# Two-layer hybrid block on one Trainium2 core: openings of both attentions and of S5's output rearranged

## What is computed

```python
# first block: one input projection, three branches, a gated merge, an MLP
proj = einsum('bld,dn->bln', rmsnorm(x), w_in)
y_a = s5_mixer(u_s5, ...)            # 32 groups: complex scan, gelu, sigmoid gate
y_b = short_conv_mixer(...)
y_c = forgetting_attention(q, k, v, f_logit, b_f)  # 8 heads, cum = cumsum(log_sigmoid(f + b_f))
merged = sum(gate_n * (y_n @ w_branch_n))
x = x + rmsnorm(merged @ w_out)
x = x + rmsnorm(square(relu(h @ w_ff1)) @ w_ff2)
# second block: one input projection, four branches, a gated merge, a SwiGLU MLP
o_a = chunk_band_attention(aq, ak, av, rel_bias)    # 4 heads, window of 576 keys
o_b = hgrn2(...);  o_c = spatial_gating(...);  o_d = rg_lru_branch(...)
```

## Time and profile before

| | |
|---|---|
| time, median of 3 executions | 3750.2 us (3750.17 to 3753.09) |
| the profiled execution | 3750.94 us, span 3749.2 us |
| TensorE matmul busy | 3518.4 us, 94% of the span |
| TensorE weight load busy | 2823.8 us, 75% |
| VectorE, ScalarE, GpSimd busy | 1434.4, 874.2, 893.5 us (38%, 23%, 24%) |
| mean granted clock of TensorE | 0.974 |
| low part of one weight unit on GpSimd (L270) | 2.48 us, mean of 276 |
| one issue of a `dl` DMA on SP (L1132) | 0.64 to 3.27 us, median 1.76 |
| issue of the first sixteen `s5_uc` loads on SP | from 88.0 us, 8.60 us long |

### The profile page before, as it was taken

How to read it: one execution, slowest core, us unless ns; L and a number is a source line. 1 busy time by engine, 2 the same in 40 slices (tenths; PEclk the granted TensorE clock), 3 DMA queues, 4 the chain that set the end, 5 groups by cost and what they waited for, 6 DMA issues and landing times. The chain is left out here.

```text
span 3749.2 us, 40647 instructions
## 1 busy us (share of the span) xinstructions
PE 3518.4 (94%) x16120; PEld 2823.8 (75%) x16120; DVE 1434.4 (38%) x1582; ACT 874.2 (23%) x1068; POOL 893.5 (24%) x421
## 2 busy tenths in 40 slices
PE   7986999999998999999988998899999899999996
PEld 4865887887885888888866887677777678888885
DVE  7713466654425212222152445562453522121123
ACT  3112222223323111111131222212232311111111
POOL 1101111111341222222321223331244222222223
PEclk9988999999999999999998999999999999999998
DMA  3335334324432111111223323213254111111122
GB/s 113 97 63 193 116 111 152 96 90 152 148 110 73 51 45 50 45 51 45 90 89 103 108 74 113 73 57 134 93 179 158 68 50 50 45 45 51 45 78 101
DMA packets 105120, 337.85 MB, mean 90 GB/s; under 512 B 15264, under 2 KB 25376, under 8 KB 104880
## 3 DMA queue, kind: packets, MB, share of 16 engines
q1 hardware_dynamic: 103520, 331.35, 27.0%
q10 hardware_dynamic: 1472, 4.72, 0.3%
HBM read 251.42 MB, written 88.67 MB: 91 GB/s over the span
## 5 line engine op out<-in xcount | busy, mean ns | idle before, releaser
L270 POOL TENSOR_TENSOR w_lo<-w_raw,w_hi 128x1024 fp32r<-128x1024 f32 x276 | 684.6, 2480 | 2502.4 <-ACT w_hi L268 2502.4
L305 PE MATMUL pair<-act_hi,w_hi 128*128 128x512 f32 x3024 | 984.5, 407 | 15.1 <-issue 7.0
L305 PE MATMUL pair<-act_lo,w_hi 128*128 128x512 f32 x3024 | 955.8, 397 | 0.0
L305 PE MATMUL pair<-act_hi,w_lo 128*128 128x512 f32 x3024 | 953.8, 396 | 0.0
L305 PEld LDWEIGHTS pair<-act_lo,w_hi 128*128 128x128 f32 x3024 | 572.4, 189 | 140.0
L305 PEld LDWEIGHTS pair<-act_hi,w_lo 128*128 128x128 f32 x3024 | 570.5, 189 | 139.9
L305 PEld LDWEIGHTS pair<-act_hi,w_hi 128*128 128x128 f32 x3024 | 553.1, 190 | 143.4 <-issue 16.5
L268 ACT CAST w_hi<-w_raw 128x1024 fp32r<-128x1024 f32 x276 | 288.9, 1047 | 770.8 <-PE pair L305 707.6
L580 DVE TENSOR_TENSOR p<-pair,rs 128x1024 f32<-128x1024 f32 x101 | 123.4, 1222 | 442.4 <-PE pair L305 436.3
L1780 DVE TENSOR_TENSOR f2v<-pair,rs 128x1024 f32<-128x1024 f32 x42 | 51.5, 1225 | 346.6 <-PE pair L305 346.6
L305 PE MATMUL pair<-f1hh,w_hi 128*128 128x512 f32 x480 | 147.8, 389 | 0.0
(11 more groups left out here) (462 smaller groups left out, 4041.5 us busy)
## 6 DMA issues: line engine op xcount, KB each, us to landing
w_raw<-in_stream SPq DMA_DIRECT2D x278, 512.0 KB, 3.6
proj<-p SPq DMA_DIRECT2D x101, 512.0 KB, 2.6
m2g<-proj SPq DMA_DIRECT2D x32, 512.0 KB, 4.8
foxx<-proj SPq DMA_DIRECT2D x32, 256.0 KB, 6.1
m1g<-proj SPq DMA_DIRECT2D x16, 512.0 KB, 3.3
x<-f1y SPq DMA_DIRECT2D x16, 512.0 KB, 2.6
act_lo<-x SPq DMA_DIRECT2D x16, 512.0 KB, 7.1
m1l<-mixed SPq DMA_DIRECT2D x12, 512.0 KB, 9.3
```

Source lines behind the costliest of these rows:

```text
L270: nc.gpsimd.tensor_tensor(wlo[:, slot, :], raw[:, slot, :], whi[:, slot, :].bitcast(F32), ALU.subtract).then_inc(s_split, 1)
L305: last = nc.tensor.matmul(out_pair[:, h * HALF:(h + 1) * HALF], wt, a[:, h * HALF:(h + 1) * HALF], start=k == 0 and n_pass == 0, stop=k == ...
```

## The change

- The copy of the input to `x0` is issued by SP within S5, right after the first sixteen loads of `s5_uc`; the two copies into spare rows are dropped, and so are the rows.
- Of the eight DMAs into `dl`, every second is issued by ScalarE (counted on `s5_in`), the others by SP, and `beside(14)` stands behind them instead of `beside(7)`.
- `beside(6)` is added ahead of the Gelus.
- `fetch(h)` waits for the three rows that it reads, not for twelve. Five points of tiles stand behind `fetch(0)` instead of two. For fox the number of points over which the tiles are spread stays `FOX_HEADS * 24 + 8`.
- In the second block 52 row blocks are one string; band begins after 25 tiles of it, without the two barriers, and its points are `BAND_HEADS * 24 + 9`. `edge` is added to the bias in `prepare(h)`. The small constants of HGRN's lower bound are made at head 2 instead of head 0.

```diff
-    def attention(heads, tiles, src, rows, mixed, row0, head_bias, add_bias, name, beside=None, closing=True):
+    def attention(heads, tiles, src, rows, stored, mixed, row0, head_bias, add_bias, name, beside=None, closing=True):
...
                 if h:
                     SP.wait_ge(*split[h - 1])
+                for n in range(3):
+                    SP.wait_ge(*stored[rows[n] + h // 2])
...
-                bias_ready[h] = bias_in(h)
+                bias_in(h)
...
                 split[h] = V.mark(V.after(a_k).tensor_tensor(ks[HD:P, sl, :], raw_qk[HD:P, 1, :],
                                                              ks[HD:P, sl, :].bitcast(F32), ALU.subtract))
+                bias_ready[h] = bias_fixed(h)
...
             fetch(0)
-            point(2)
+            point(5)
             prepare(0)
             point(2)
             state["copied"] = values(0, None)
...
-        for row in range(Q_, F_):
-            SP.wait_ge(*stored[row])
...
             edge = sb(outer, "bd_edge", [P, BAND])
-            barrier()
-
             G.mark(G.then().memset(edge[:], 0.0))
             G.mark(G.then().memset(edge[0:64, LEFT + 64:], -1e30))
-            G.mark(G.then().memset(edge[64:P, 0:64], -1e30))
-            barrier()
+            edged = G.mark(G.then().memset(edge[64:P, 0:64], -1e30))
+            G.then()
...
-                def ready(h):
-                    got = bias_load[h % 2].mark(SP.dma_start(rel[:, h % 2, :], t["rel"][h]))
-                    return V.mark(V.after(got).tensor_tensor(rel[:, h % 2, :], rel[:, h % 2, :], edge[:], ALU.add))
-                return rel, ready
+                def fetched(h):
+                    bias_load[h % 2].mark(SP.dma_start(rel[:, h % 2, :], t["rel"][h]))
+
+                def fixed(h):
+                    return V.mark(V.after(bias_load[h % 2].last(), edged).tensor_tensor(rel[:, h % 2, :], rel[:, h % 2, :],
+                                                                                        edge[:], ALU.add))
+                return rel, fetched, fixed
...
             chunks(0)
             chunks(1)
+            x0_out.mark(SP.dma_start(x0, x_in))
...
-            SP.wait_ge(*v)
-            SP.wait_ge(*zeroed)
+            for queue in (SP, nc.scalar):
+                queue.wait_ge(*v)
+                queue.wait_ge(*zeroed)
             for j in range(T):
-                dl_in.mark(SP.dma_start(dl[j * S5_H:(j + 1) * S5_H, :, j * S5_H:].rearrange("p g (a b) -> p g a b", b=S5_H),
-                                        kc[:, :, 0:T - j, :]))
-            w.beside(7)
+                queue, arrived = ((SP, dl_in), (nc.scalar, s5_in))[j % 2]
+                arrived.mark(queue.dma_start(dl[j * S5_H:(j + 1) * S5_H, :, j * S5_H:].rearrange("p g (a b) -> p g a b", b=S5_H),
+                                             kc[:, :, 0:T - j, :]))
+            w.beside(14)
...
             w.beside(5)
+            w.beside(6)
             gelus = [A.mark(A.after(u_in[n].last()).activation(z[n], z[n], ACT.Gelu_apprx_tanh)) for n in range(4)]
...
-            if head == 0:
+            if head == 2:
...
             w.upto(17 * KT + 1)
-            for spare, d in enumerate((proj1[N1], proj2[N2])):
-                stores[spare].mark(SP.dma_start(d, x_in[0]))
-            x0_copied = x0_out.mark(SP.dma_start(x0, x_in))
             w.again(FOX_HEADS * 24 + 8, KT)
...
-        stored = {}
-        stage(2, 2, 2, KT, act_rhs, to_dram(proj2, AQ + 2, buf), per=out_per)
-        barrier()
+        stored = {row: outs[row - AQ].last() for row in (AQ, AQ + 1)}
...
-        with Woven(products(0, used["units"], 48, 48, KT, act_rhs, evict), 48 * KT, 1) as w:
+        with Woven(products(0, used["units"], 52, 52, KT, act_rhs, evict), 52 * KT, 1) as w:
             with ExitStack() as early:
                 hgrn_const, constants_beside = hgrn_constants(early)
-                w.again(BAND_HEADS * 24 + 6, 32 * KT)
-                band(constants_beside)
+                w.upto(3 * KT + 1)
+                w.again(BAND_HEADS * 24 + 9, 32 * KT)
+                band(constants_beside, stored)
```

More of the change, by code:

```diff
@@ L669, in attention @@
             st = sb(at, name + "st", [P, 2, 1])
-            bias, bias_in = head_bias(at)
+            bias, bias_in, bias_fixed = head_bias(at)
             G.mark(G.then().memset(vt[:, :, 0, :, HD:], 1.0))
@@ L796, in head_bias @@
             cb = sb(at, "fx_cb", [P, 2, L])
-            return cb, lambda h: bias_load[h % 2].mark(SP.dma_start(cb[:, h % 2, :], fox_cum[h].partition_broadcast(P)))
+            def fetched(h):
+                bias_load[h % 2].mark(SP.dma_start(cb[:, h % 2, :], fox_cum[h].partition_broadcast(P)))
+            return cb, fetched, lambda h: bias_load[h % 2].last()
         def add_bias(sc, psum, cb, q0, k0, k1):
@@ L802, in add_bias, with band, fetched @@
             return v
[L804 to L805 removed]
         with ExitStack() as at:
[L807 removed]
+            attention(FOX_HEADS, [(n * P, 0, (n + 1) * P) for n in range(8)], proj1, (Q_, K_, V_), stored, mixed1, 8,
                       head_bias, add_bias, "fox", short_conv(at, stored), closing=False)
[L810 removed]
+    def band(beside, stored):
         with ExitStack() as outer:
             edge = sb(outer, "bd_edge", [P, BAND])
[L814 removed]
             G.mark(G.then().memset(edge[:], 0.0))
             G.mark(G.then().memset(edge[0:64, LEFT + 64:], -1e30))
[L818 to L819 removed]
+            edged = G.mark(G.then().memset(edge[64:P, 0:64], -1e30))
+            G.then()
             def head_bias(at):
                 rel = sb(at, "bd_rel", [P, 2, BAND])
[L824 to L827 removed]
+                def fetched(h):
+                    bias_load[h % 2].mark(SP.dma_start(rel[:, h % 2, :], t["rel"][h]))
[3 more added lines that the diff above has]
+                return rel, fetched, fixed
             def add_bias(sc, psum, rel, q0, k0, k1):
@@ L833, in band @@
             attention(BAND_HEADS, [(n * P, max(0, n * P - LEFT), (n + 1) * P) for n in range(8)], proj2,
-                      (AQ, AK, AV), mixed2, 0, head_bias, add_bias, "band", beside, closing=False)
+                      (AQ, AK, AV), stored, mixed2, 0, head_bias, add_bias, "band", beside, closing=False)
     def s5(w, stored):
@@ L1140, in s5 @@
                 ps = sides[n % 2]
-                PE.after(states, dl_in.last(), *copied[n % 2])
+                PE.after(states, dl_in.last(), s5_in.last(), *copied[n % 2])
                 for pr in range(p0, p0 + 4):
@@ L1235, in beside @@
                 V.mark(V.then().tensor_scalar(oml, x, -1.0, 1.0, ALU.mult, ALU.add))
-                return
-            for n in range(3 * head - 3, min(3 * head, LEVELS)):
+            for n in range(max(0, 3 * head - 3), min(3 * head, LEVELS)):
                 w = P >> (n + 1)
@@ L1890, in _build @@
         late = Late(at, "f1")
-        SP.wait_ge(*x0_copied)
+        SP.wait_ge(*x0_out.last())
         mix_out(late, x0, "g_post_mix", x1, "g_pre_mlp", first_hidden(late, False))
@@ L1898, in _build @@
         buf = sb(at, "p2", [P, 2, L])
-        stored = {}
-        stage(2, 2, 2, KT, act_rhs, to_dram(proj2, AQ + 2, buf), per=out_per)
-        barrier()
+        stored = {row: outs[row - AQ].last() for row in (AQ, AQ + 1)}
         def evict(i, o, psum, ready, read):
-            to_dram(proj2, BQ, buf)(i, o, psum, ready, read)
-            stored[BQ + o] = outs[o % 2].last()
-        with Woven(products(0, used["units"], 48, 48, KT, act_rhs, evict), 48 * KT, 1) as w:
+            to_dram(proj2, AK, buf)(i, o, psum, ready, read)
+            stored[AK + o] = outs[o % 2].last()
+        with Woven(products(0, used["units"], 52, 52, KT, act_rhs, evict), 52 * KT, 1) as w:
             with ExitStack() as early:
                 hgrn_const, constants_beside = hgrn_constants(early)
-                w.again(BAND_HEADS * 24 + 6, 32 * KT)
-                band(constants_beside)
+                w.upto(3 * KT + 1)
+                w.again(BAND_HEADS * 24 + 9, 32 * KT)
+                band(constants_beside, stored)
                 w.again(140, 12 * KT)
@@ L1920, in _build @@
             next(merging)
-        advance(48, 48)
+        advance(52, 52)
         next(merging)
```

5 lines of the change are left out of this document (1 added, 4 removed).

## The result

| | before | after |
|---|---|---|
| median (lowest to highest of 4) | 3751.64 us (3750.17 to 3759.67) | 3716.81 us (3709.99 to 3721.03) |
| ratio, 95% interval | | 0.9901, 0.988 to 0.9922 |
| profiled execution, span | 3750.94, 3749.2 us | 3717.39, 3715.7 us |
| TensorE busy | 3518.4 us | 3521.0 us |
| mean granted clock | 0.974 | 0.977 |

What follows compares the result with a forecast made beforehand. TensorE was taken to bound the kernel, with its waits and slow clock. Gains of 18.2, 9.8, 19.2 and 22.1 less 1.8 gave 67.5 us, so 3750.2 became 3683 us; range 3674 to 3700.

Steps and rivals of the forecast that it cites:

- S5's output: Products behind the dl factors: the 9.7 us wait and the slow clock behind it go, gaining 18.2 us.
- I take no wait, because even a small speed-up closes 2.7 us: At the dl factors: two queues land them early enough to remove the 2.7 us left if the split gave nothing.
- covered, with 1.6 us to spare: ScalarE's four issues (7.2 us), then cast and low part end near 221; TensorE needs that weight unit at 222.6.
- Rival 1: At the dl factors: ScalarE's queue delays its cast, TensorE waits 5.5 us, clock falls; 14.0 us lost, 3697; chance 0.14.
- The gates: S5's gates: four more tiles and an earlier Gelu remove the 8.4 us wait and 1.4 of slow clock, gaining 9.8 us.
- Fox's opening: The wait for v falls from 20.0 to 1.8 us; with clock effects, 19.2 us gained.
- 3.0 us later: Fox's opening: last S5 store, issued at G + 7.5 (G: fourth gate product's start), lands 3.0 us later; barrier opens G + 10.6.
- rival 2: Fox's opening: loads come 6 us later than forecast, costing 6 us of wait and 1 of clock; 3690; chance 0.14.
- Fox's body and end: Tiles run out before fox's last query tile, uncovering two waits for ScalarE copies; costs 1.8 us.
- tiles moved cost nothing: Rule for the whole sum: tiles done elsewhere take the same 1.4 us each; only waits and clock count.
- Band: Band's opening: waits of 8.9 us for v and 9.5 behind VectorE shrink, two slow stretches go; 22.1 us gained.
- What stays is the normal step: Band's second wait, 9.5 us behind VectorE, shrinks to the usual 0.7 us between query tiles.

Runs made afterwards that it cites:

- SP held: The changed kernel with SP made to wait until all eight dl factors have landed before its next store and weight load: 3699.14 us (ratio 0.9859).
- one queue and 18 us: The changed kernel with all eight dl DMAs on SP again and `beside(18)` instead of `beside(14)` behind them: 3683.41 us (ratio 0.9819).
- the kernel with band's bias first: The one queue and 18 us kernel with band's first bias loaded ahead of q and k and its edge added before they come: 3680.44 us (0.9805).

## Why the prediction was wrong

- **S5's output, 18.2, got 4**, and, with what it moves elsewhere, nothing in the time. The step that failed is "I take no wait, because even a small speed-up closes 2.7 us". No run shows a speed-up: with SP held the last factor lands 16.7 us after the first issue, and one queue does it in 16.6 to 17.8. I costed SP's four issues at half of eight and forgot what SP does when it is free: its next stores and weight load run among the outstanding factors, and the last one lands 3.7 us later. The second failure is that I priced the 2.7 us that might be left at their length: at this place waits of 2.5 and 3.4 us brought the 1.2 GHz back nearly in full. The size of the prize was right (8.4 and 2.8 us when nothing waits), the condition for it was not. ScalarE's "covered, with 1.6 us to spare" was wrong by 3.4 us: issues of 10.43 instead of 7.2 us, wait 1.8. Rival 1 had this mechanism, at 5.5 us; the larger part came by a way that neither it nor the forecast had.
- **The gates, 9.8, got 10.** Right in size. The reason was half right: the earlier load does all of it, the gates' own tiles nothing. And the load is early because of the tiles behind the `dl` DMAs, so this gain hangs on the term above, which the sum took as separate.
- **Fox's opening, 19.2, got 15.5.** Loads to v took 8.3 us, as the earlier trace rows said. The step that failed is the "3.0 us later" for the last S5 store. It was issued at G + 7.8, about as forecast, landed 5.1 us later and the barrier opened 5.7 us later. SP's timeline of the changed kernel:

```profile
325.69 0.32 SPq L582 DMA_DIRECT2D proj<-p  x1
326.75 0.33 SPq L275 DMA_DIRECT2D w_raw<-in_stream  x1
327.12 0.47 SPq L1223 DMA_DIRECT2D mixed<-s_state  x1
332.79 2.44 SPq L685 DMA_DIRECT2D foxx<-proj  x4
```

  Two 512 KB transfers stand just ahead of the store. Without them the same store landed in 2.6 us (the kernel without the gates' tiles); no run takes them away alone. The wait was 4.5 us instead of 1.8. This was rival 2, at half its size.
- **Fox's body and end, -1.8, got -6.2.** The last query tile lost its tiles and waited 0.77 and 0.67 us, as forecast. What failed is the premise that tiles moved cost nothing: a second head met GpSimd's split. Waits in fox's stretch grew from 10.6 to 14.6 us, and the slow clock in it from 3.4 to 5.1.
- **Band, 22.1, got 12.5 (13.9 alone).** v was right: 0.4 us where I had none. "What stays is the normal step" failed: 3.6 us and the slow stretch behind it stayed, since the add of 0.82 us lasted 2.86 beside GpSimd and an eviction queued behind it; and band's body is 2.5 us slower than its three tiles more account for.
- The misses add up: 14.2 + 3.7 + 4.4 + 9.6 = 31.9 of 33.8 us. That the terms fit so well is in part luck, with one traced execution on each side.
- "Five stand out, and all five lie at the three places of this change" passes over a wait of 14.3 us behind ScalarE's `n1s` (L351), in the norm, which this change doesn't touch. It changes no term.

What stays open: what costs the 4 us behind band, what in fox besides the long subtraction a shift of three tiles takes away, and why a wait of 3 us there is sometimes followed by 1.2 GHz and sometimes not. Removing GpSimd's split from VectorE's way, rather than moving tiles until they miss each other, was not tried.

## What to carry to other kernels

When transfers are split over two queues, list what each queue issues next: large transfers behind the short half delay the other half. Closing most of a wait gives back its length but not the clock, if the clock falls behind what is left; add tiles until nothing is left (on one queue the first five tiles, 7.0 us of the wait, gave 7.4 us, which is barely beyond noise, and the next three 25.8, about half of it in fox). Moving tiles also moves the evictions, casts and loads that come with every eighth, and so changes terms elsewhere; price the places together. In a woven kernel, look where each two-input VectorE instruction falls against GpSimd's, since a shift of three tiles was worth more than most of the planned edits.

## What the hardware showed

- Four issues of short packets took ScalarE 10.43 us while SP's four took 7.20; the eight together on SP take 14.26. The Trainium skill (DMA: Bandwidth & Descriptors, Issuing engines are not separate DMA queues) says that transfers issued from several engines share the same 16 DMA engines and that only the issue time is saved. The traces agree: the last factor lands 16.7 us after the first issue from two queues with SP held, and 16.6 to 17.8 from one. Once SP goes on, it is 20.4 to 21.5.
- In S5's output, after waits of 2.5, 3.4 and 9.7 us, TensorE ran these 128-column products at 0.50 for much of the next 15 us though busy throughout; after none, at 1.00. In fox waits of 2.9 to 3.0 us were followed by 0.50 in some traces and by 1.00 in others, at the same place of the program. Summed over windows of 2.5 us from 100 to 2300 us, busy time times (1 - PEclk) is 33.7 us before, 34.6 after, 17.3 with one queue and 18 us.
- VectorE's instruction that begins while GpSimd's split runs ends about its own length after the split: 3.28 instead of 1.22, 2.86 instead of 0.82. In the other order GpSimd gives way: the subtraction at 342.4 in the changed kernel takes 1.22 us, and the split that begins within it 2.88 instead of 2.48. The eviction, which has an input in PSUM, is not held (in the changed kernel seven begin within a GpSimd instruction and take 1.22 or 1.23 us): 1.23 us at 1956.78, within this split of the kernel with band's bias first (GpSimd's timeline):

```profile
1956.21 2.77 POOL L270 TENSOR_TENSOR w_lo<-w_raw,w_hi 128x1024 fp32r<-128x1024 f32 x1 [11.37 <-ACT w_hi L268]
```
